# A two-network kernel at batch 1: x is loaded first and split before the decay constants, bias rows are loaded one at a time, and the last retention head is computed one weight tile earlier

## The chip, the cores and the metric

The kernel runs on one core of one Trainium2 chip. PE is the matrix engine, DVE the vector engine, ACT the scalar (activation) engine, POOL (GpSimd) and SP only issue DMAs here, apart from a few fills at the start. The metric is the device time of one execution in microseconds (us); lower is better. Of the kernel before there are three timed runs and one profiled execution.

## The reference

Two networks run one after the other on x of 256 tokens by 1024, all in float32. Cut to what the change touches:

```python
x = first_block(x, ...)    # layer 0: retention + FFN, layer 1: dilated attention + FFN
x = second_block(x, ...)   # two layers, with a recurrence whose decay is
                           # exp(-8 * r * softplus(-rg_lambda))

def retention(x, w_in, w_out):                 # 4 heads, q/k 256 wide, v 512 wide
    q, k, v, gate = split(x @ w_in)
    q, k = rope(q), rope(k) * 256 ** -0.5
    y = (q @ k.T * decay[head]) @ v            # per head, causal, over 256 tokens
    y = (y - mean(y)) * rsqrt(var(y) + 1e-5)   # over the 512 of a head
    return (silu(gate) * y) @ w_out

def dilated_attention(x, w_in, w_out, rel_bias):   # 3 groups x 16 heads of 64
    s = q @ k.T * 64 ** -0.5 + bias[group, head, distance]   # T5 buckets of rel_bias
    ...
```

`-8 * softplus(-rg_lambda)` depends on weights alone; the text calls it the decay constants (`rate` in the kernel). It is first used in the second network, some 1500 us later.

## The kernel before, in words

All weights form one stream of tiles of 512 KB (128 x 1024 float32), 878 in all, in the order of use. SP loads tile b into slot b % 4 of `raw` (L275, L297) as soon as tile b - 4 has been split. ACT rounds it to `wh` (`hi`, L397), DVE forms the rest `wl = raw - wh` (`lo`, L863), each with two buffers, and PE multiplies in three passes (high x high, high x low, low x high; L1534 to L1536), so that a float32 product comes of fast passes. `hi(b)` waits until tile b - 2 has been used on PE. Activations are split in the same way, x into `xh` and `xl`.

The order on each engine is that in which the code is written: every engine runs its own program and waits on semaphores. A piece of work that is late holds back all that is written behind it on its engine. There is no scheduler.

**Start.** POOL issues the loads of constants (`cst`, with the identity), vectors (`vec`: gains, biases, lambda) and x (L331 to L333); SP issues the first four raw tiles at once. PE transposes x in 16 pieces (L1663) and then the gain rows of `vec` (L1665), and goes on to the value tiles of retention, the first of which waits for half of `xl`. ACT splits tiles 0 and 1, takes an exponential for the decay constants and rounds x (L480). DVE begins with three tiny operations on constants and vectors, splits tiles 0 and 1, computes the decay constants in a chain of 26 operations of 128 x 4 (a series of odd powers, L971 to L981), and only then forms `xl` (L986).

**Retention heads.** The 16 gate tiles (n = 0 to 15) run through PE, and between them stand the heads' own products: `ret_scores(h)` (L1685), `ret_values(h)` (L1699, L1700) and the sum of squares `ret_var(h)` (L1708), in a period of three tiles. With them go on DVE `ret_decay` (L1026), `ret_recip` (L1031), `ret_gate` (L1036) and `ret_scale` (L1042), on ACT `ret_square` (L500) and `ret_std` (L504). For the last head DVE multiplies the products by the reciprocal as L1077 and by the gate as L1081. The output tiles that follow need all PSUM banks of the products, so PE waits for L1077 before the first of them (`r_yg`).

**Bias rows of attention.** PE forms the bias rows of all heads, POOL stores them in DRAM (L352) and loads them back head by head, shifted by one per partition (L358, 384 KB each), into four buffers. The first four loads wait only for the store and for the norm before; each later one waits for a used buffer (`a_b`). Meanwhile 24 value tiles of the attention stage pass through PE; they are loaded in pieces of 1 KB. The first bias is used after the tile at offset 30 of the stage.

Of the kernel before, what the change touches and what calls it, by code (L numbers as in the profile page):

```python
# [93 lines left out]
def build(nc, stream, x_in, consts, ret_c, att_c, vecs, rg_w, keys, scratch, out):  # L94
    with ExitStack() as ctx:
# [121 lines left out]
        const_in, x_in_s, retc_in, attc_in = sem("const_in"), sem("x_in"), sem("retc_in"), sem("attc_in")  # L217
# [55 lines left out]
        def _(sp):  # L273
# [18 lines left out]
            def in_parts(first, parts):  # L292

                for b, (g, part) in enumerate(parts, first):
                    if b >= 4:
                        sp.wait_ge(w_lo, b - 3)
                    sp.dma_start(raw[:, b % 4, :].rearrange("p (m n) -> p m n", m=4),  # L297
# [32 lines left out]
        def _(pool):  # L330
            pool.dma_start(cst[:, :], consts).then_inc(const_in, 16)  # L331
            pool.dma_start(vec[:, :], vecs).then_inc(const_in, 16)
            pool.dma_start(xr[:, :, :], x_in.rearrange("(c p) d -> p c d", p=P)).then_inc(x_in_s, 16)  # L333
            pool.wait_ge(x_turned, 1)
# [20 lines left out]
            for h in range(AH):  # L355
                if h >= 4:
                    pool.wait_ge(a_b, h - 3)
                pool.dma_start(bs[:, h % 4, :, :], bass.AP(  # L358
                    scratch.tensor, h * 384, [[1, P], [AH * 384, G3], [1, T]])).then_inc(b_in[h % 4], 16)
# [20 lines left out]
        def _(act):  # L380
# [92 lines left out]
            act.wait_ge(const_in, 32)  # L473
            hi(0)
            hi(1)
            act.wait_ge(sp_abs, 1)
            A(spw[:, 2, :], spw[:, 1, :], ACT.Exp, scale=-1.0).then_inc(sp_exp, 1)
            act.wait_ge(x_turned, 1)
            for g in range(4):
                A(xh[:, 2 * g:2 * g + 2, :], acc[:, 2 * g:2 * g + 2, :], ACT.Copy).then_inc(x_hi, 1)  # L480
            act.wait_ge(rows_in_vec, 1)
            A(vec_rows[0:104, :], ps_x[0:104, 0, 0:P], ACT.Copy).then_inc(rows_copied, 1)

# [23 lines left out]
            for n in range(16):  # L507
                hi(RET_G + n + 2)
                evacuate(RET_G + n, 16 + n, sg[:, n, :], ACT.Silu)
                if n >= 3 and n % 3 == 0 and n < 15:  # L510
                    ret_square(n // 3 - 1)
                elif n >= 4 and n % 3 == 1 and n < 15:
# [334 lines left out]
        def _(dve):  # L847
# [115 lines left out]
            dve.wait_ge(const_in, 32)  # L963
# [4 lines left out]
            lo(0)  # L968
            lo(1)
# [13 lines left out]
            for g in range(4):  # L983
                dve.wait_ge(x_hi, g + 1)
                b = slice(2 * g, 2 * g + 2)
                V.tensor_tensor(xl[:, b, :], acc[:, b, :], xh[:, b, :].bitcast(F32), ALU.subtract).then_inc(x_lo, 1)  # L986
# [62 lines left out]
            for n in range(16):  # L1049
# [3 lines left out]
                elif n in (2, 5, 8, 11):  # L1053
# [16 lines left out]
                elif n == 12:  # L1070
                    ret_gate(2)
                    ret_scale(2)
                elif n == 14:
                    ret_recip(3)
                elif n == 15:
# [452 lines left out]
        def _(pe):  # L1528
# [130 lines left out]
            pe.wait_ge(const_in, 32)  # L1659
# [545 lines left out]
```

## Time and profile before

| | us |
|---|---|
| median of 3 timed runs | 2948.59 |
| lowest and highest | 2946.07, 2948.68 |
| the profiled execution | 2945.24 |
| its span (first to last instruction) | 2943.5 |
| PE busy | 2817.1 (96%) |
| DVE busy, ACT busy | 1941.7, 1557.4 |
| mean granted clock of PE | 0.989 |

The page gives an engine's busy time, the chain of work that ended last, and groups of instructions by line. A timeline row is one or several equal instructions in a row, with the idle time before them in brackets and what ended it. A released wait is put down to the last event that was needed. The granted clock is a share of 2.4 GHz; it has two levels here, 1.0 and 0.5.

### The profile page before, as it was taken

Reading aid. Unit: us, or ns where it says so; the run is one execution under the profiler, and the core shown is the slowest. Engines: PE = TensorE matmul, PEld = TensorE weight load, DVE = VectorE, ACT = ScalarE, POOL = GpSimd, SP = SyncE. Lnnn points to the kernel's source line nnn. Section 1 sums busy time; section 2 is a strip of 40 time slices with the busy share of each in tenths; the row PEclk is TensorE's granted clock in tenths of the full one; section 3 lists DMA queues with packets and bytes.
Section 4 is the critical chain, followed back from the end, with each engine's and each line's share of the span. In section 5 each row is a group of like instructions: output and inputs, shape, how many; then the busy total and the mean of one; then the engine's idle time right before and its main releaser. Section 6 shows DMA issues by size and latency. Waiting matters only on the chain.

```text
span 2943.5 us, 51574 instructions
## 1 busy us (share of the span) xinstructions
PE 2817.1 (96%) x18787; PEld 2548.3 (87%) x18787; DVE 1941.7 (66%) x3107; ACT 1557.4 (53%) x2815; POOL 23.0 (1%) x38
## 2 busy tenths in 40 slices
PE   8999999999999989999999999998999999999998
PEld 6988987898898879999998888887999999978886
DVE  5656454555555869986886555568799678855555
ACT  4455453555545564446775444456544577644444
POOL 0000000000000000000000000000000000000000
PEclk9999999999999999999999999999999999999999
DMA  6435556664554444454444555543444444455554
GB/s 219 151 130 183 185 170 180 172 159 149 165 184 159 133 130 164 158 170 143 138 144 144 192 190 189 191 161 109 163 161 163 159 140 143 138 178 192 190 189 149
DMA packets 158659, 480.26 MB, mean 163 GB/s; under 512 B 14608, under 2 KB 51472, under 8 KB 158128
## 3 DMA queue, kind: packets, MB, share of 16 engines
q1 hardware_dynamic: 154080, 460.38, 47.4%
q0 software_dynamic: 4432, 17.87, 2.6%
q8 instruction: 98, 1.61, 0.2%
q14 instruction: 49, 0.40, 0.0%
HBM read 477.02 MB, written 1.18 MB: 162 GB/s over the span
## 4 chain that ended last, share of the span: by engine, by line
PE 77%; DVE 16%; ACT 4%; issue 2%; DMA 1%; POOL 0%; DVEq 0%; ACTq 0%; POOLq 0%
PE ps L1534 23%; PE ps L1536 23%; PE ps L1535 23%; DVE wl L863 6%; PE ps L2049 4%; ACT wh L397 2%; DVE arena L1251 1%; DVE mh L1404 1%; DVE picks L1406 1%; DVE mh L1398 1%; PE ps L1653 1%; DMA raw<-stream_dram 1%; DVE xr L882 0%; PE ps L2015 0%; DVE picks L1428 0%
## 5 line engine op out<-in xcount | busy, mean ns | idle before, releaser
L863 DVE TENSOR_TENSOR wl<-raw,wh 128x1024 fp32r<-128x1024 f32 x878 | 1075.5, 1225 | 889.6 <-ACT wh L397 883.6
L397 ACT ACTIVATE wh<-raw 128x1024 fp32r<-128x1024 f32 x878 | 929.9, 1059 | 1281.8 <-PE ps L1536 1270.9
L1534 PE MATMUL ps<-xh,wh 128*128 128x256 f32 x3920 | 1138.9, 291 | 24.4 <-DVE wl L863 22.9
L1535 PE MATMUL ps<-xl,wh 128*128 128x256 f32 x3920 | 1111.5, 284 | 0.0
L1536 PE MATMUL ps<-xh,wl 128*128 128x256 f32 x3920 | 1110.9, 283 | 0.0
L1534 PEld LDWEIGHTS ps<-xh,wh 128*128 128x128 f32 x3920 | 753.4, 192 | 49.2 <-issue 36.9
L1535 PEld LDWEIGHTS ps<-xl,wh 128*128 128x128 f32 x3920 | 754.6, 193 | 0.4
L1536 PEld LDWEIGHTS ps<-xh,wl 128*128 128x128 f32 x3920 | 753.7, 192 | 0.0
L1534 PE MATMUL ps<-wh,mh 128*128 128x512 f32 x1304 | 516.6, 396 | 13.7 <-DVE ml L875 8.8
L1536 PE MATMUL ps<-wh,ml 128*128 128x512 f32 x1304 | 512.1, 393 | 0.0
L1535 PE MATMUL ps<-wl,mh 128*128 128x512 f32 x1304 | 511.0, 392 | 0.0
L1534 PEld LDWEIGHTS ps<-wh,mh 128*128 128x128 f32 x1304 | 246.0, 189 | 90.9 <-issue 33.3
L1536 PEld LDWEIGHTS ps<-wh,ml 128*128 128x128 f32 x1304 | 246.0, 189 | 54.2
L1535 PEld LDWEIGHTS ps<-wl,mh 128*128 128x128 f32 x1304 | 246.7, 189 | 43.5
L411 ACT ACTIVATE arena<-ps 128x256 f32<-128x256 f32 (+1 forms) x360 | 132.2, 367 | 0.2
L1534 PE MATMUL ps<-wh,xh 128*128 128x512 f32 x248 | 101.4, 409 | 15.5 <-DVE wl L863 5.7
L875 DVE TENSOR_TENSOR ml<-arena,mh 128x512 fp32r<-128x512 f32 x158 | 108.1, 686 | 4.4 <-ACT mh L443 4.4
L443 ACT ACTIVATE mh<-arena 128x512 fp32r (+1 forms) x158 | 96.9, 615 | 7.1 <-DVE arena L1494 3.9
L1494 DVE TENSOR_TENSOR arena<-arena,ps 128x260 f32<-128x260 f32 (+42 forms) x128 | 71.1, 556 | 42.7 <-ACT arena L817 40.9
L1535 PE MATMUL ps<-wl,xh 128*128 128x512 f32 x248 | 98.8, 398 | 0.0
L1536 PE MATMUL ps<-wh,xl 128*128 128x512 f32 x248 | 98.4, 397 | 0.0
L797 ACT ACTIVATE picks<-mh,pickT 128x128 f32<-128x128 f32 x256 | 81.5, 398 | 4.4 <-DVE mh L1482 4.4
(280 smaller groups left out, 2040.1 us busy)
## 6 DMA issues: line engine op xcount, KB each, us to landing
raw<-stream_dram SPq DMA_DIRECT2D x878, 512.0 KB, 3.3
arena<-bias_scratch POOLq DMA_DIRECT2D x16, 384.0 KB, 9.8
arena<-norm_rows POOLq DMA_DIRECT2D x4, 1024.0 KB, 6.8
arena<-keys_dram POOLq DMA_DIRECT2D x2, 1024.0 KB, 5.1
arena<-ret_c_dram POOLq DMA_DIRECT2D x1, 1344.0 KB, 6.1
xr<-x_dram POOLq DMA_DIRECT2D x1, 1024.0 KB, 9.2
out_dram<-arena POOLq DMA_DIRECT2D x2, 512.0 KB, 2.9
arena<-rg_w_dram POOLq DMA_DIRECT2D x2, 256.0 KB, 2.9
```

The source lines that it names most:

```text
L397: A(wh[b % 2][:, :, :], raw[:, b % 4, :].rearrange("p (a b) -> p a b", a=DB), ACT.Copy) \
L411: A(dst, src, func, scale=scale, **kw).then_inc(evac, 1)
L443: A(mh[:, s:s + 2, :], src, ACT.Copy).then_inc(m_hi, 1)
L797: ins = A(gated[n % 3][:, j, :], oh[n % 2][:, j, :].bitcast(F32), ACT.Copy, scale=gT[:, t:t + 1])
L863: V.tensor_tensor(wl[b % 2][:, :, :], raw[:, b % 4, :].rearrange("p (a b) -> p a b", a=DB), wh[b % 2][:, :, :].bitcast(F32), ALU.subtract) ...
L875: V.tensor_tensor(ml[:, s:s + 2, :], src, mh[:, s:s + 2, :].bitcast(F32), ALU.subtract) \
L1251: ins = V.scalar_tensor_tensor(out=cy[:, b, :], in0=src, scalar=vec[:, w:w + 1], in1=cy[:, b, :], op0=ALU.mult, op1=ALU.add)
L1494: V.tensor_tensor(h, h, ps_a[:, n % 4, :].rearrange("p (t m) -> p m t", t=4)[:, 0:known, :], ALU.mult).then_inc(g_mul, 1)
L1534: M(out_ap, lh, rh, start=first, stop=False, skip_group_check=skip)
L1535: M(out_ap, lh, rl, start=False, stop=False, skip_group_check=skip)
L1536: return M(out_ap, ll, rh, start=False, stop=last, skip_group_check=skip)
L2049: ins = M(ps_a[:, n % 4, j * P:(j + 1) * P], gated[n % 3][:, j, :], oh[n % 2][:, 4 + j, :].bitcast(F32), start=True, stop=True)
```

## The change

Three parts.

1. x is the first load that POOL issues, the vectors the second; ACT issues the constants. Raw tiles 2 and 3 wait until x has landed. PE transposes x block by block (both token halves of a block of 128 columns in turn) and signals after each pair of blocks; ACT and DVE split x pair by pair. DVE splits tiles 0 and 1 first, then does its three small operations, then `xl`, and then the decay constants. The retention constants are loaded after the whole transposition, as before. Constants and vectors have semaphores of their own.
2. The first four bias loads wait for the split of tile 12, 16, 20 and 24 of the attention stage (counted from its start).
3. For the last retention head, scores, decay, products, square, variance, deviation, reciprocal and product stand one gate tile earlier than before.

```diff
@@ SP
                     if b >= 4:
                         sp.wait_ge(w_lo, b - 3)
+                    elif b == 2:
+                        sp.wait_ge(x_in_s, 16)
@@ POOL
-            pool.dma_start(cst[:, :], consts).then_inc(const_in, 16)
-            pool.dma_start(vec[:, :], vecs).then_inc(const_in, 16)
             pool.dma_start(xr[:, :, :], x_in.rearrange("(c p) d -> p c d", p=P)).then_inc(x_in_s, 16)
-            pool.wait_ge(x_turned, 1)
+            pool.dma_start(vec[:, :], vecs).then_inc(vec_in, 16)
+            pool.wait_ge(x_turned, 4)
             pool.dma_start(rc, ret_c).then_inc(retc_in, 16)
...
                 if h >= 4:
                     pool.wait_ge(a_b, h - 3)
+                else:
+                    pool.wait_ge(w_lo, START["att"] + 12 + 4 * h)
@@ ACT
-            act.wait_ge(const_in, 32)
+            act.dma_start(cst[:, :], consts).then_inc(const_in, 16)
             hi(0)
             hi(1)
-            act.wait_ge(sp_abs, 1)
-            A(spw[:, 2, :], spw[:, 1, :], ACT.Exp, scale=-1.0).then_inc(sp_exp, 1)
-            act.wait_ge(x_turned, 1)
             for g in range(4):
+                act.wait_ge(x_turned, g + 1)
                 A(xh[:, 2 * g:2 * g + 2, :], acc[:, 2 * g:2 * g + 2, :], ACT.Copy).then_inc(x_hi, 1)
             act.wait_ge(rows_in_vec, 1)
             A(vec_rows[0:104, :], ps_x[0:104, 0, 0:P], ACT.Copy).then_inc(rows_copied, 1)
+            act.wait_ge(sp_abs, 1)
+            A(spw[:, 2, :], spw[:, 1, :], ACT.Exp, scale=-1.0).then_inc(sp_exp, 1)
...
-                if n >= 3 and n % 3 == 0 and n < 15:
-                    ret_square(n // 3 - 1)
-                elif n >= 4 and n % 3 == 1 and n < 15:
+                if n in (3, 6, 9, 11):
+                    ret_square((n - 1) // 3)
+                elif n in (4, 7, 10, 12):
                     ret_std(n // 3 - 1)
@@ DVE
+            lo(0)
+            lo(1)
+            dve.wait_ge(const_in, 16)
+            dve.wait_ge(vec_in, 16)
...
-            lo(0)
-            lo(1)
+            for g in range(4):
+                dve.wait_ge(x_hi, g + 1)
+                b = slice(2 * g, 2 * g + 2)
+                V.tensor_tensor(xl[:, b, :], acc[:, b, :], xh[:, b, :].bitcast(F32), ALU.subtract).then_inc(x_lo, 1)
             dve.wait_ge(sp_exp, 1)
...
-            for g in range(4):
-                dve.wait_ge(x_hi, g + 1)
-                b = slice(2 * g, 2 * g + 2)
-                V.tensor_tensor(xl[:, b, :], acc[:, b, :], xh[:, b, :].bitcast(F32), ALU.subtract).then_inc(x_lo, 1)
...
-                elif n in (2, 5, 8, 11):
+                elif n in (2, 5, 8, 10):
                     ret_decay(n // 3)
...
-                elif n == 14:
+                elif n == 13:
                     ret_recip(3)
-                elif n == 15:
+                elif n == 14:
                     y3 = ry[:, 12:16, :]
...
@@ PE
-            for c in range(NC_T):
-                for b in range(DB):
+            for b in range(DB):
+                for c in range(NC_T):
                     ins = nc.tensor.transpose(acc[:, b, c * P:(c + 1) * P], xr[:, c, b * P:(b + 1) * P], ident)
-            ins.then_inc(x_turned, 1)
+                if b % 2:
+                    ins.then_inc(x_turned, 1)
+            pe.wait_ge(vec_in, 16)
             nc.tensor.transpose(ps_x[0:104, 0, 0:P], vec[:, 0:104], ident).then_inc(rows_in_vec, 1)
...
-                if n >= 4 and n % 3 == 1:
+                if n in (4, 7, 10, 12):
                     ret_var(n // 3 - 1)
-                elif n >= 3 and n % 3 == 0 and n < 15:
-                    ret_values(n // 3 - 1)
-                elif n >= 2 and n % 3 == 2 and n < 14:
+                elif n in (3, 6, 9, 11):
+                    ret_values((n - 1) // 3)
+                if n in (2, 5, 8, 10):
                     ret_scores(n // 3)
```

What stands in a row on the engines follows, with the waits of each instruction in brackets; "x3" is three equal instructions. Line numbers of the kernel after differ a little: L863 is L866 there.

On DVE, at the start, before: the end of the decay constants (L979 to L981), the four pieces of `xl` (L986), and the weight splits from tile 2 on (L863).

```order
L979 TENSOR_TENSOR arena<-arena 128x4 [waits dve_step]
L980 TENSOR_SCALAR arena<-arena 128x4 [waits dve_step]
L981 SCALAR_TENSOR_TENSOR rate<-arena 128x4 [waits dve_step]
L986 TENSOR_TENSOR xl<-ps,xh 128x512 [waits x_hi,dve_step]
L986 TENSOR_TENSOR xl<-ps,xh 128x512 [waits x_hi] x3
L863 TENSOR_TENSOR wl<-raw,wh 128x1024 [waits w_hi] x4
```

After: tiles 0 and 1 (L866), the three small operations (L970 to L973), the four pieces of `xl` (L977), and the first of the decay constants.

```order
L866 TENSOR_TENSOR wl<-raw,wh 128x1024 [waits w_hi] x2
L970 TENSOR_TENSOR head_rows<-cst 128x8 [waits vectors_in,const_in]
L972 TENSOR_SCALAR arena<-vec 128x4
L973 TENSOR_TENSOR arena<-arena,vec 128x4 [waits dve_step]
L977 TENSOR_TENSOR xl<-ps,xh 128x512 [waits x_hi] x4
L979 TENSOR_SCALAR arena<-arena 128x4 [waits rate_exp]
L980 RECIPROCAL arena<-arena 128x4 [waits dve_step]
L981 TENSOR_TENSOR arena<-arena 128x4 [waits dve_step]
```

And where the decay constants end, the weight split of tile 2 follows them:

```order
L987 TENSOR_TENSOR arena<-arena 128x4 [waits dve_step]
L988 TENSOR_SCALAR arena<-arena 128x4 [waits dve_step]
L989 SCALAR_TENSOR_TENSOR rate<-arena 128x4 [waits dve_step]
L866 TENSOR_TENSOR wl<-raw,wh 128x1024 [waits w_hi,dve_step]
L866 TENSOR_TENSOR wl<-raw,wh 128x1024 [waits w_hi] x3
```

So `xl` has moved ahead of the chain, and the split of tile 2 (L866, waiting on `dve_step`, the chain's own semaphore) now stands right behind it.

On DVE at the last gate tiles, before: the weight splits of steps n = 10 and 11 (L863 x2; step n splits the tile two ahead, gate tile n + 2), and so on to L1081, the product with the gate of the last head.

```order
L863 TENSOR_TENSOR wl<-raw,wh 128x1024 [waits w_hi] x2
L1026 TENSOR_TENSOR arena<-ps,arena 128x384 [waits ret_y,ret_scores]
L1031 RECIPROCAL arena<-arena 128x256 [waits ret_std]
L863 TENSOR_TENSOR wl<-raw,wh 128x1024 [waits w_hi,dve_step]
L1036 TENSOR_TENSOR arena<-ps,arena 128x1024 [waits evac,ret_y]
L1042 TENSOR_TENSOR arena<-arena 128x1024 [waits ret_gated]
L863 TENSOR_TENSOR wl<-raw,wh 128x1024 [waits w_hi] x2
L1031 RECIPROCAL arena<-arena 128x256 [waits ret_std]
L863 TENSOR_TENSOR wl<-raw,wh 128x1024 [waits w_hi,dve_step]
L1077 TENSOR_TENSOR arena<-ps,arena 128x1024
L1081 TENSOR_TENSOR arena<-arena 128x1024 [waits ret_gated,evac]
```

After, from the last head's decay (L1030, before L1026) on; L1035 is the reciprocal, L1081 and L1085 are the two products of the last head (before L1077 and L1081).

```order
L1030 TENSOR_TENSOR arena<-ps,arena 128x384 [waits ret_y,ret_scores]
L866 TENSOR_TENSOR wl<-raw,wh 128x1024 [waits w_hi]
L1035 RECIPROCAL arena<-arena 128x256 [waits ret_std]
L866 TENSOR_TENSOR wl<-raw,wh 128x1024 [waits w_hi,dve_step]
L1040 TENSOR_TENSOR arena<-ps,arena 128x1024 [waits evac,ret_y]
L1046 TENSOR_TENSOR arena<-arena 128x1024 [waits ret_gated]
L866 TENSOR_TENSOR wl<-raw,wh 128x1024 [waits w_hi]
L1035 RECIPROCAL arena<-arena 128x256 [waits ret_std]
L866 TENSOR_TENSOR wl<-raw,wh 128x1024 [waits w_hi,dve_step]
L1081 TENSOR_TENSOR arena<-ps,arena 128x1024
L866 TENSOR_TENSOR wl<-raw,wh 128x1024 [waits w_hi]
L1085 TENSOR_TENSOR arena<-arena 128x1024 [waits ret_gated,evac]
```

The last head's decay stands before the split of step 11 instead of behind it, its reciprocal before the split of step 14 (gate tile 16, which is the first output tile) instead of behind it, and its first product before the split of step 15 (tile 17) instead of behind it.

On POOL around the bias rows, before: the store of the rows (L352), the 16 loads (L358), and the gain rows of the next norms (L339).

```order
L352 DMA bias_scratch<-arena 16x3x384 [waits bias_vec_copied]
L358 DMA arena<-bias_scratch 128x3x256 [waits norm_updated,bias_stored]
L358 DMA arena<-bias_scratch 128x3x256 x3
L358 DMA arena<-bias_scratch 128x3x256 [waits att_biased] x12
L339 DMA arena<-norm_rows 128x2x1024 [waits att_biased,norm_updated]
```

After:

```order
L353 DMA bias_scratch<-arena 16x3x384 [waits bias_vec_copied]
L361 DMA arena<-bias_scratch 128x3x256 [waits w_lo,norm_updated,bias_stored]
L361 DMA arena<-bias_scratch 128x3x256 [waits w_lo] x3
L361 DMA arena<-bias_scratch 128x3x256 [waits att_biased] x12
L340 DMA arena<-norm_rows 128x2x1024 [waits att_biased,norm_updated]
```

The first four loads have each got a wait on the weight splits (`w_lo`); the order is the same.

## Rows read from the trace of the kernel before

**Rows 1.** The page: span, and the chain that ended last by engine.

```profile
span 2943.5 us, 51574 instructions
...
PE 77%; DVE 16%; ACT 4%; issue 2%; DMA 1%; POOL 0%; DVEq 0%; ACTq 0%; POOLq 0%
```

**Rows 2.** Timeline, 0 to 20 us: start, duration, engine, line, operation [idle before, releaser].

```profile
1.28 0.70 POOL L331 DMA_DIRECT2D cst<-consts_dram  x1 [0.83 <-POOLq L2197]
...
2.52 0.73 POOL L333 DMA_DIRECT2D xr<-x_dram  x1
...
11.72 0.16 DVE L971 TENSOR_SCALAR arena<-arena 128x4 f32<-128x4 f32 x1
...
11.86 3.65 PE L1663 MATMUL ps<-cst,xr 128*128 128x128 f32 x16 [11.86 <-DMA xr<-x_dram]
...
15.55 2.07 ACT L480 ACTIVATE xh<-ps 128x512 fp32r<-128x512 f32 x4 [5.09 <-PE ps L1663]
...
16.66 0.16 DVE L981 SCALAR_TENSOR_TENSOR rate<-arena 128x4 f32<-128x4 f32 x1
...
16.85 2.48 DVE L986 TENSOR_TENSOR xl<-ps,xh 128x512 fp32r<-128x512 f32 x4
...
18.29 0.47 PE L1534 MATMUL ps<-wh,xh 128*128 128x512 f32 x1 [2.56 <-DVE xl L986]
```

**Rows 3.** Timeline of PE, 22.3 to 28 us: third tile's first product.

```profile
25.46 0.40 PE L1534 MATMUL ps<-wh,xh 128*128 128x512 f32 x1
```

**Rows 4.** DMA, 0 to 60 us: GB/s in slices; loads, KB, us to landing.

```profile
GB/s 0 165 377 380 361 393 389 349 321 204 175 115 366 432 40 44 360 287 308 176 212 180 172 219 140 268 104 307 96 268 107 245 136 216 253 102 307 98 279 57
...
xr<-x_dram POOLq DMA_DIRECT2D x1, 1024.0 KB, 9.2
...
arena<-norm_rows POOLq DMA_DIRECT2D x1, 1024.0 KB, 5.4
```

**Rows 5.** Groups of PE by line: count, busy us, mean ns, idle before.

```profile
L1818 PE MATMUL ps<-cst,arena 128*128 128x128 f32 x16 | 4.4, 273 | 0.0
...
L1663 PE MATMUL ps<-cst,xr 128*128 128x128 f32 x16 | 3.6, 423 | 11.9 <-DMA xr<-x_dram 11.9
```

**Rows 6.** Stretches: busy (count) of PE, PEld, DVE, ACT, POOL; clock, DMA, GB/s.

```profile
189.84:193.26 3.42, 3.24 (x8) 2.59 (x9) 1.30 (x2) 0.00 (x0) 0.00 (x0) 0.51 0.47 153
...
479.97:483.40 3.43, 3.43 (x8) 2.76 (x9) 1.63 (x2) 0.07 (x1) 0.00 (x0) 0.51 0.53 170
```

**Rows 7.** Timeline, 184 to 191 us: the last head and the first output tile.

```profile
185.76 1.75 DVE L1031 RECIPROCAL arena<-arena 128x256 f32<-128x256 f32 x1
...
187.56 1.23 DVE L863 TENSOR_TENSOR wl<-raw,wh 128x1024 fp32r<-128x1024 f32 x1
...
188.70 1.22 DVE L1077 TENSOR_TENSOR arena<-ps,arena 128x1024 f32<-128x1024 f32 x1
...
190.02 0.76 PE L1534 MATMUL ps<-wh,mh 128*128 128x512 f32 x1 [3.71 <-issue]
```

**Rows 8.** Timeline, 455 to 500 us: bias loads, and the value tiles of attention.

```profile
460.88 3.01 POOL L358 DMA_DIRECT2D arena<-bias_scratch  x4 [3.12 <-DMA bias_scratch<-arena]
...
479.92 0.80 PE L1534 MATMUL ps<-wh,xh 128*128 128x512 f32 x1 [5.73 <-DVE wl L863]
...
485.70 1.23 DVE L863 TENSOR_TENSOR wl<-raw,wh 128x1024 fp32r<-128x1024 f32 x1 [4.11 <-ACT wh L397]
...
488.42 1.23 DVE L863 TENSOR_TENSOR wl<-raw,wh 128x1024 fp32r<-128x1024 f32 x1 [1.49 <-ACT wh L397]
```

**Rows 9.** DMA, 460 to 480 us: queues (packets, MB, share); raw tiles' landing.

```profile
q0 software_dynamic: 456, 1.58, 40.1%
...
q1 hardware_dynamic: 2614, 2.60, 39.9%
...
raw<-stream_dram SPq DMA_DIRECT2D x6, 512.0 KB, 11.1
```

**Rows 10.** DMA, 545 to 575 us: raw tiles' landing.

```profile
raw<-stream_dram SPq DMA_DIRECT2D x7, 512.0 KB, 3.8
```

More of the change, by code:

```diff
@@ L216, in build @@
         m_hi, m_lo = sem("m_hi"), sem("m_lo")
-        const_in, x_in_s, retc_in, attc_in = sem("const_in"), sem("x_in"), sem("retc_in"), sem("attc_in")
+        const_in, vec_in, x_in_s, retc_in, attc_in = sem("const_in"), sem("vectors_in"), sem("x_in"), sem("retc_in"), sem("attc_in")
         x_turned, x_hi, x_lo = sem("x_turned"), sem("x_hi"), sem("x_lo")
@@ L960, in norm @@
                         updated(c)
-            dve.wait_ge(const_in, 32)
+            lo(0)
+            lo(1)
+            dve.wait_ge(const_in, 16)
+            dve.wait_ge(vec_in, 16)
             V.tensor_tensor(head_rows[:, :], ident[:, 0:H2], ident[:, 32:32 + H2], ALU.add).then_inc(rows_in, 1)
@@ L1072, in _ @@
                     ret_scale(2)
+                elif n == 13:
+                    ret_recip(3)
                 elif n == 14:
-                    ret_recip(3)
-                elif n == 15:
                     y3 = ry[:, 12:16, :]
@@ L1656, in norm @@
                             ins.then_inc(n_turned, 1)
-            pe.wait_ge(const_in, 32)
+            pe.wait_ge(const_in, 16)
             pe.wait_ge(x_in_s, 16)
-            for c in range(NC_T):
-                for b in range(DB):
+            for b in range(DB):
+                for c in range(NC_T):
                     ins = nc.tensor.transpose(acc[:, b, c * P:(c + 1) * P], xr[:, c, b * P:(b + 1) * P], ident)
-            ins.then_inc(x_turned, 1)
+                if b % 2:
+                    ins.then_inc(x_turned, 1)
+            pe.wait_ge(vec_in, 16)
             nc.tensor.transpose(ps_x[0:104, 0, 0:P], vec[:, 0:104], ident).then_inc(rows_in_vec, 1)
```

## The prediction

> **What bounds the kernel now.** I read the page first: its chain of work that ended last lies on PE for 77% of the span and on DVE for 16%, and the profiled execution has a span of 2943.5 us [rows 1]. So only time in which PE stands still, or runs at half its clock, can be won here; nothing in the change takes a product away. Then I read the timelines at the three places that the change touches, with the DMA view beside them.
>
> At the start x lands at 2.52 + 9.2 = 11.7 us, PE transposes from 11.86, and its first product against weights begins at 18.29, released by the split of x on DVE. That split (xl, 16.85) stands behind a chain of tiny operations, the decay constants (11.72 to 16.82, 5.1 us). The third weight tile begins at 25.46 [rows 2, 3]. At the end of the retention stage PE waits 3.71 us, until 190.02, for the last head's product L1077 on DVE, which stands behind a reciprocal and a weight split [rows 7]. In the attention stage PE waits 5.73 us, until 479.92, for a weight split whose raw tile was late: four loads of bias rows had gone out together at 460.88, and raw tiles issued in that stretch took 11.1 us to land, against 3.8 later [rows 8 to 10]. Behind both waits lie 3.4 us at a granted clock of 0.51, which is the level of 1.2 GHz, half of 2.4 [rows 6].
>
> **The change, part by part.**
>
> *x first.* Before x has landed, 4 raw tiles of 512 KB, 328 KB of constants, 138 KB of vectors and 1024 KB of x are moved: 3538 KB, 3.62 MB. The slices of 1.5 us show 361 to 393 GB/s [rows 4]; at 380 that is 9.5 us, and with the first bytes at about 2.2 us it gives 11.7, as measured. Now raw tiles 2 and 3 wait for x, so 2376 KB (2.43 MB) stand before it: 6.4 us, 8.6. The vectors now follow x and may share its last stretch (0.14 MB, 0.4 us). I take 8.9. Bounds: with the issue alone moved (from 2.52 to 1.28, where the constants' issue stood [rows 2]) and nothing of the crowd gone, 10.5; with no crowd at all, 1.28 + 5.4 (the 1024 KB load of the gain rows [rows 4]) = 6.7.
>
> Some edits here I cost at nothing. The constants' load is issued by ACT, which otherwise waits for the first raw tile; it has 4 us before PE wants it. Raw tiles 2 and 3 go out at 9 and land by about 13 to 14, and nobody can use them before tile 0 is done, at 15.6 or later. Queued behind the waiting issue on SP are tiles 4 and 5, which are wanted after 20. The 1344 KB load of the retention constants follows the last transposition as before. The vectors gate the first DVE operation after the weight splits and the last transposition; they must be there by about 10.5, else the whole split of x moves with them.
>
> *The split before the decay constants.* From x at 8.9: 16 transpositions 3.65 us [rows 2], 9.0 to 12.65. ACT and DVE now follow in four pieces (0.52 and 0.62 us each, from 2.07 and 2.48 for four [rows 2]); the last piece ends on ACT at 13.2 and on DVE at 13.95. PE begins tile 0 at 12.9, after the turned vectors. On ACT a copy of the vector rows (104x128) and an exponential (128x4) follow, both small beside its 0.52. Then DVE runs the decay constants, 14.0 to 19.1, and only behind them the low half of tile 2, 1.23 us, 20.3. Tiles 0 and 1 are done at 12.9 + 2 x 2.72 = 18.4 (2.72 is one tile: 488.42 - 485.70 [rows 8]). So tile 2 begins at 20.4 instead of 25.46 [rows 3]: the start gains 5.1 us, and a new wait of about 2 us stands where the chain was moved to. Without it the gain would be 7.1.
>
> The 16 transpositions have a mean of 423 ns, the same form later 273 [rows 5], so the start is at the low level. If tile 0 is too, it costs up to 1.7 us, but inside the wait of 2 us, nothing. The Trainium skill, "TensorE: Matmul & The Clock Gate", Part 1, says that the throttled clock is the default and that activity releases it, and that the phase differs from run to run. The two means agree; by that rule the remaining wait may be followed by a slow stretch in some executions and not in others.
>
> *The last head one tile forward.* Scores, products and variance of head 3 go behind tiles 10, 11 and 12 instead of 11, 12 and 13. PE does the same work up to 186.3. On DVE the reciprocal (1.75 us, 185.76 [rows 7]) moves ahead of tile 16's split, and L1077 takes the place at 185.76; it takes 1.22, so PE can begin at about 187.1. The wait shrinks from 3.71 to 0.8: 2.9 us. With a wait of 0.8 the half-clock stretch should go: 190.02 to 193.26 at half is 3.24 us that do the work of 1.6. Sum 4.5. What is late next: tile 17's split keeps its 187.56 to 188.8 [rows 7], and the second output tile wants it at 187.1 + 2.72 = 189.8; it holds. Bounds: 0 if the moved reciprocal meets a late variance, 5.3 if L1077 is ready when PE is.
>
> *Bias rows one by one.* The four loads took 40.1% of 20 us of all 16 DMA engines, 2.0 us each [rows 9]. A raw tile is asked for when the split four tiles earlier is done, 1.23 us after that split began; ACT wants it 1.1 us before its own split begins. Four tiles are 10.9 us, so it has 10.9 - 1.2 - 1.1 = 8.6 us to land. With 11.1 it was late; with 3.8 to 4 [rows 10] and one bias load of 2.0 in its way it takes about 6. One load in four tiles also fits in sum: 2.0 + 4 x 1.6 (a raw tile's share, from 2.60 MB in 39.9% of 20 us [rows 9]) = 8.4 of 10.9 us. The first row set is loaded 18 tiles before its use, the fourth 6 tiles, 16 us. So the wait of 5.73 goes and with it the half-clock stretch, 3.43 us that do 1.7: 7.4 us. Bounds: if the four still make raw tiles late by a little each, I keep half, 3.7; more than 7.4 isn't there.
>
> **Sum.** 5.1 + 4.5 + 7.4 = 17.0, less 0.8 for half a chance of a slow stretch behind the new wait at 20.4: 16.2. Against the profiled execution, 2945.24 (span 2943.5 and 1.7 around it), that is 2929.0; the median of the runs shown is 3.35 higher, 2948.59, which gives 2932.4. I take 2931.
>
> **The rivals.** *x lands without a crowd*, at 6.7: everything at the start, the decay chain too, comes 2.2 earlier, 2929. For it: ACT and SP use one queue kind and x another. Against: the 9.2 us it took in company. The Trainium skill, "DMA: Bandwidth & Descriptors", Anatomy of one DMA, fits a load from this queue as 2.0 us and the bytes at 436 GB/s, 4.4 for x; by it alone x would be there at 5.7 and the whole come to about 2928 (an estimate from that page), and only the 5.4 row comes near it.
>
> *The head's wait only moves.* Two groups of products now stand behind tile 10, and DVE has decay, reciprocal, product and scaling within three tiles. If one of these makes PE wait as long as before, 4.5 is lost: 2935.5. Against it: DVE's work between two of these tiles is 3 to 4 us, and the tiles with products behind them are 4.5 to 6 us apart.
>
> *The attention wait stays or is spread* over the four bias loads: 3.7 to 7.4 are lost, 2935 to 2938.
>
> *Slower: each bias load stalls PE for itself.* If one load of 2.0 us among raw tiles makes the tile behind it land later than 8.6 us, and each of the four does what the group did, that is 4 x 7.4 = 29.6 in place of the one 7.4 gone: 2960. It decides at 8.6 us of landing. Against it is the 3.8 while bias loads went out in pairs [rows 10]. If it is only one of four, the time is about 2938.
>
> *x isn't earlier than its issue* (10.5, or the vectors late): 1.6 less, 2932.5; it lies inside my forecast's scatter.
>
> **How the numbers follow.** Forecast (both x cases at the start included) 0.66, its own range 2926 to 2936. x without a crowd 0.08. Head's wait moves 0.09. Attention wait stays or is spread 0.12. Slower 0.05. The range of 8 in 10: from 2925 (all three waits gone and x early) to 2940 (the attention gain lost, from the higher median: 2932.4 + 7.4). 0.2% is 5.9 us, about what a measurement of this kernel can tell from no change. Faster by more, under 2942.7: all but the last case and a rest for two terms failing together, 0.90; within, 0.06; slower, 0.04.
>
> **What would show it.** In the profile after: x landing near 8.9; the first weight product near 12.9; a wait of about 2 us at the third tile, released by a weight split that follows the decay chain; at the output tiles of retention a wait under 1 us, with the clock at 1.00; no wait of PE over 1 us in the value tiles of attention, and raw tiles landing under 8.6 us there. Wrong would be the forecast if x lands after 10.5, if PE waits between gate tiles 10 and 14, or if the value tiles have waits on a weight split behind each bias load.

## The result, and the profile after

The kernel after takes 2930.48 us (median of 4 runs, 2929.25 to 2931.00) against 2947.33 of the kernel before (4 runs, 2945.87 to 2948.68) on the same chip: the ratio is 0.9942, with a 95% interval of 0.9931 to 0.9954, or 16.9 us. Forecast were 2931, and faster by 16.2 us. The two profiled executions are 2945.24 and 2930.42 us, 14.8 apart.

The page of the kernel after:

```profile
span 2928.6 us, 51574 instructions
...
PE 77%; DVE 16%; ACT 4%; issue 2%; DMA 1%; DVEq 0%; ACTq 0%; POOL 0%; POOLq 0%
```

It answers to [rows 1]: the shares of the chain are the same to the percent, and only the span has shrunk, by 14.9 us. A gain of 0.5% isn't seen in shares; it is seen where rows of one and the same piece of work are set side by side.

The timeline of the kernel after at the start, against [rows 2, 3] (start, duration, engine, line, operation; idle before and its end in brackets):

```profile
1.29 0.85 POOL L333 DMA_DIRECT2D xr<-x_dram  x1 [0.83 <-POOLq L2203]
...
9.47 3.65 PE L1667 MATMUL ps<-cst,xr 128*128 128x128 f32 x16 [9.47 <-DMA xr<-x_dram]
...
12.98 0.78 PE L1538 MATMUL ps<-wh,xh 128*128 128x512 f32 x1
...
14.39 0.16 DVE L979 TENSOR_SCALAR arena<-arena 128x4 f32<-128x4 f32 x1
...
19.33 0.16 DVE L989 SCALAR_TENSOR_TENSOR rate<-arena 128x4 f32<-128x4 f32 x1
19.52 2.36 DVE L866 TENSOR_TENSOR wl<-raw,wh 128x1024 fp32r<-128x1024 f32 x2
...
20.80 0.50 PE L1538 MATMUL ps<-wh,xh 128*128 128x512 f32 x1 [1.70 <-DVE wl L866]
```

x is issued at 1.29, PE transposes from 9.47 instead of 11.86, the first weight product comes at 12.98 instead of 18.29 and the third tile at 20.80 instead of 25.46. In front of it stands the new wait, 1.70 us, on the weight split at 19.52, and that follows the end of the decay constants (19.33) directly. In the kernel before the first tile had run for the most part at half clock, behind the wait of 2.56 us, and had taken 4.41 us (18.29 to 22.70):

```profile
19.12:22.54 3.42, 3.42 (x10) 2.65 (x9) 0.21 (x1) 0.00 (x0) 0.21 (x1) 0.50 0.61 251
```

Now it takes 3.24 us. The 4.7 us of the start are thus 5.3 at the first product and 1.2 in the first tile, less the new wait of 1.7 and 0.1. DMA in the first 60 us, against [rows 4]:

```profile
GB/s 0 170 379 384 396 388 6 255 381 343 354 416 430 165 105 321 283 303 261 338 304 170 297 107 299 61 294 159 193 145 206 236 141 270 115 281 46 322 197 156
...
xr<-x_dram POOLq DMA_DIRECT2D x1, 1024.0 KB, 8.1
...
cst<-consts_dram ACTq DMA_DIRECT2D x1, 328.0 KB, 3.2
```

The seventh slice (9 to 10.5 us) moves next to nothing: SP issues its third raw tile only at 9.35, when x is there, and POOL waits for the transposition. x took 8.1 us in place of 9.2.

The end of retention in the kernel after, against [rows 7]; L1035 is the reciprocal, L1081 the first product of the last head:

```profile
178.67 1.75 DVE L1035 RECIPROCAL arena<-arena 128x256 f32<-128x256 f32 x1
...
180.47 1.23 DVE L866 TENSOR_TENSOR wl<-raw,wh 128x1024 fp32r<-128x1024 f32 x1
...
181.61 1.22 DVE L1081 TENSOR_TENSOR arena<-ps,arena 128x1024 f32<-128x1024 f32 x1
...
182.93 0.47 PE L1538 MATMUL ps<-wh,mh 128*128 128x512 f32 x1 [0.49 <-issue]
```

The wait of PE is 0.49 us instead of 3.71. The stretch behind it, of which [rows 6] show the like before, is at full clock:

```profile
182.93:186.30 3.37, 3.37 (x15) 2.78 (x16) 2.36 (x2) 1.21 (x3) 0.00 (x0) 1.00 0.50 159
```

The attention stage, POOL's issues and then PE, against [rows 8]:

```profile
465.77 0.79 POOL L361 DMA_DIRECT2D arena<-bias_scratch  x1 [16.38 <-DVE wl L866]
476.75 0.76 POOL L361 DMA_DIRECT2D arena<-bias_scratch  x1 [10.19 <-DVE wl L866]
487.73 0.76 POOL L361 DMA_DIRECT2D arena<-bias_scratch  x1 [10.22 <-DVE wl L866]
498.83 0.76 POOL L361 DMA_DIRECT2D arena<-bias_scratch  x1 [10.34 <-DVE wl L866]
```

```profile
508.13 1.06 ACT L400 ACTIVATE wh<-raw 128x1024 fp32r<-128x1024 f32 x1 [2.59 <-DMA raw<-stream_dram]
...
510.50 0.50 PE L1538 MATMUL ps<-wh,xh 128*128 128x512 f32 x1 [0.64 <-DVE wl L866]
```

The four loads now stand 11 us apart and the wait of 5.73 us is gone. One of 0.64 is left, behind the fourth load: the raw tile of 508.13 came late (ACT waited 2.59 us for it). Issued at 498.55, 0.3 us before the fourth bias load, it took 9.6 us. Raw tiles of 490 to 510 us landed after 6.7 us (median of 7), between the 11.1 of [rows 9] and the 3.8 of [rows 10].

**Where the 14.9 us of the profiled pair lie.** One fixed point is POOL's first pair of later bias loads, issued when two heads have used theirs: 548.45 before, 533.56 after:

```profile
548.45 1.49 POOL L358 DMA_DIRECT2D arena<-bias_scratch  x2 [84.55 <-DVE arena L1157]
```

```profile
533.56 1.51 POOL L361 DMA_DIRECT2D arena<-bias_scratch  x2 [33.98 <-DVE arena L1161]
```

The kernel after is 14.9 us ahead there, as much as at its end. In between the distance isn't constant: it goes up to 18.5 and down to 13.7, mostly in steps of about 1.5 us (more on them under order_only). Set side by side by the order number of the PE product, the two traces give the steps: 4.7 at the third tile, 4.2 from tile 14 on (a wait of 0.25 us has come there), 8.5 behind the retention stage, 15.9 behind the big attention wait, 14.9 at the fixed point.

### The profile page after: what moved, and what is told of

Read it like the earlier page. It is cut to its first block, busy times and chain, and to the rows that moved or that the text cites. A ratio compares the mean times of both kernels' runs of the same rounds, so it can differ in the third digit from the quotient of the medians.

```text
span 2928.6 us, 51574 instructions
## 1 busy us (share of the span) xinstructions
PE 2813.6 (96%) x18787; PEld 2545.0 (87%) x18787; DVE 1941.9 (66%) x3107; ACT 1557.9 (53%) x2815; POOL 22.7 (1%) x37
## 4 chain that ended last, share of the span: by engine, by line
PE 77%; DVE 16%; ACT 4%; issue 2%; DMA 1%; DVEq 0%; ACTq 0%; POOL 0%; POOLq 0%
PE ps L1538 23%; PE ps L1540 23%; PE ps L1539 23%; DVE wl L866 6%; PE ps L2055 4%; ACT wh L400 2%; DVE arena L1255 1%; DVE mh L1408 1%; DVE picks L1410 1%; DVE mh L1402 1%; DVE xr L885 0%; PE ps L2021 0%; DVE picks L1432 0%; DVE picks L1440 0%; DVE picks L1423 0%
## 5 line engine op out<-in xcount | busy, mean ns | idle before, releaser
L866 DVE TENSOR_TENSOR wl<-raw,wh 128x1024 fp32r<-128x1024 f32 x878 | 1075.6, 1225 | 881.6 <-ACT wh L400 875.1
L1538 PE MATMUL ps<-wh,mh 128*128 128x512 f32 x1304 | 515.2, 395 | 10.5 <-DVE ml L878 8.8
```

What stands on the lines that cost most here:

```text
L866: V.tensor_tensor(wl[b % 2][:, :, :], raw[:, b % 4, :].rearrange("p (a b) -> p a b", a=DB), wh[b % 2][:, :, :].bitcast(F32), ALU.subtract) ...
L1538: M(out_ap, lh, rh, start=first, stop=False, skip_group_check=skip)
```

## The experiments

All run against the kernel before on their own chip. The medians scatter by some us (those of the kernel before are 2947.33, 2948.33, 2949.90 and 2950.81), so beside each ratio I give the place in the profiled execution at which the edit acts.

**only_start, only_head, only_bias: each part alone.** The kernel before with one of the three parts of the diff shown above, and nothing else.

> The kernel before with part 1 alone (x first, raw tiles 2 and 3 behind x, split before the decay constants). Theory (the three gains are separate and add up): the third weight tile begins at 20.8 us as in the kernel after instead of 25.46, 0.4 of the 4.7 us is lost by tile 14, so the time is 4.2 us under the kernel before; the waits at the head (3.7 us) and in the attention values (5.7 us) stay as they were. Rival (the start sets the phase of everything that follows, and much of the 16.9 us hangs on it): over 8 us faster, with one of the two later waits changed by more than 1 us.

> The kernel before with part 3 alone (last head one tile earlier). Theory: the wait before the first output tile of retention falls from 3.71 to 0.5 to 0.8 us and the half-clock stretch behind it goes; 4.3 to 4.5 us faster. Rival (the half-clock stretch hangs on the time since the start and not on the wait): the wait goes and the stretch stays, 2.9 us faster.

> The kernel before with part 2 alone (each of the first four bias loads behind a weight split). Theory: the wait of 5.73 us and the 3.4 us at half clock behind it go, 7.4 us, of which 1.0 comes back as small waits near the fourth load: 6.4 us faster. Rival (in the kernel after some of this gain came from the other parts, since the stage begins 8.5 us earlier there): under 4 us faster, with a wait over 2 us left in the value tiles.

Ratios 0.9988 (0.9979 to 0.9997), 0.9978 (0.9968 to 0.9988) and 0.9977 (0.9968 to 0.9986): 3.5, 6.5 and 6.8 us, each with an interval of nearly 3 us to either side, sum 16.8, against 17.1 for all three by 0.9942. The places, in this order: PE at the third tile in only_start, PE at the first output tile in only_head, and all waits of PE in the stretch of 440 to 545 us in only_bias.

```profile
20.67 0.50 PE L1536 MATMUL ps<-wh,xh 128*128 128x512 f32 x1 [1.29 <-DVE wl L864]
```

```profile
186.86 0.47 PE L1534 MATMUL ps<-wh,mh 128*128 128x512 f32 x1 [0.49 <-issue]
```

```profile
PE ps L1804 <- DVE arena L1153: 0.7, 1, 0.7
PE ps L1791 <- DVE arena L997: 0.3, 1, 0.3
```

The start gives 4.8 us at the third tile and 4.4 at the end of its stage; the waits at 181.9 (3.72 us) and 469.6 (4.60) stay in only_start. The head's wait falls to 0.49, and no half-clock stretch follows: 4.3 us are won over that stage. In only_bias no wait on a weight split is left in the value tiles; 7.6 us are won over them, and 0.5 given back. Over their own stages the three are 4.4, 4.3 and 7.6 us, against 4.2, 4.3 and 7.6 in the kernel after: the gains are separate and add up. At the fixed point the three kernels are 5.1, 4.4 and 7.6 us ahead, 2.2 more in sum than the kernel after; of these, 0.8 came to only_start behind its own stage, and 1.2 is what the kernel after gives back behind the retention stage. The rivals fall, with one exception in part: in only_start the wait in the attention values was 1.1 us shorter than before, with the same loads, so the size of that wait itself varies from execution to execution.

**bias_together_late: four loads at once, but later.**

```diff
-                    pool.wait_ge(w_lo, START["att"] + 12 + 4 * h)
+                    pool.wait_ge(w_lo, START["att"] + 12)
```

> The kernel after, but all four first bias loads wait for the same split, that of tile 12 of the attention stage, and so go out together 17 us later than in the kernel before. Theory (four at once crowd out the raw tiles, whenever it is): a PE wait of 4 to 6 us returns behind them, with half clock behind it, raw tiles land after 10 us; 6 to 7 us slower than the kernel after, about 2937. Rival (what helped was that the loads no longer fall on the first value tiles, right behind the store of the rows): no wait over 1 us, the time of the kernel after, 2930.

2940.78 us in its one run. Waits of PE, 440 to 540 us, and the loads issued from 465 to 485 us:

```profile
PE ps L1538 <- DVE wl L866: 7.0, 1, 7.0
```

```profile
raw<-stream_dram SPq DMA_DIRECT2D x5, 512.0 KB, 13.1
arena<-bias_scratch POOLq DMA_DIRECT2D x4, 384.0 KB, 9.9
```

The wait is back, 7.0 us, and raw tiles took 13.1 us. It is the four together that crowd out the raw tiles, not the place in the stage. By 540 us this kernel has lost 8.3 us of the 14.9. Expected had been a wait of 4 to 6 us and about 2937: the direction was right, the price too low.

**raw_not_held: raw tiles 2 and 3 don't wait for x.**

```diff
-                    elif b == 2:
-                        sp.wait_ge(x_in_s, 16)
```

> The kernel after without the wait of raw tiles 2 and 3 on x: all four raw tiles are issued at once again, x is still POOL's first load. Theory (bytes ahead of x set its landing): 1.05 MB more at 380 GB/s, x lands 2.8 us later than the 9.4 of the kernel after, about 12.2 less what x's own turn among the queues gives back, and the third weight tile begins 2 to 2.8 us later; 2932 to 2933. Rival (x is bound by its own queue, not by the others' bytes): x lands at 9.4 as before and the time stays 2930.

2931.20 us, one run. PE in this kernel, and x's load:

```profile
10.07 3.57 PE L1665 MATMUL ps<-cst,xr 128*128 128x128 f32 x16 [10.07 <-DMA xr<-x_dram]
...
21.33 0.51 PE L1536 MATMUL ps<-wh,xh 128*128 128x512 f32 x1 [2.12 <-DVE wl L864]
```

```profile
xr<-x_dram POOLq DMA_DIRECT2D x1, 1024.0 KB, 8.6
```

x is there 0.6 us later, not 2.8, and took 8.6 us in place of 8.1, although 1.05 MB more were under way. So the sum of bytes ahead of x, on which I had the landing, isn't what sets it: x shares with the raw tiles and isn't behind all of them. The kernel before shows it too: its fourth raw tile, issued at 2.33 and counted ahead of x in the prediction, took 10.7 us and landed at 13.0, behind x. What brought x forward from 11.86 to 9.47 is mostly its place as the first load of its queue (1.23 us by the issue, 2.52 to 1.29), with 0.6 for the held tiles; the remaining 0.6, for what no longer stands ahead of it in that queue, is only what is left over. The 0.6 for the held tiles rests on one execution: in six kernels with all of part 1's loads the transposition begins between 9.33 and 9.78, in four with the old loads between 11.51 and 11.86, and 10.07 lies 0.3 outside the first group.

**order_only: the order of work alone, all loads as before.**

```diff
-            pool.dma_start(xr[:, :, :], x_in...).then_inc(x_in_s, 16)
-            pool.dma_start(vec[:, :], vecs).then_inc(vec_in, 16)
+            pool.dma_start(cst[:, :], consts).then_inc(const_in, 16)
+            pool.dma_start(vec[:, :], vecs).then_inc(vec_in, 16)
+            pool.dma_start(xr[:, :, :], x_in...).then_inc(x_in_s, 16)
```

(against only_start; ACT issues nothing and SP holds nothing back)

> The kernel before with only the order of the work at the start changed (PE signals pairs of blocks, ACT and DVE split x ahead of the decay constants), while all loads are issued where they were in the kernel before. Theory (landing of x and order of work each give about half of the start's 4.7 us): x lands at 11.7 as before, the third weight tile begins 11.4 us behind it (the distance in the kernel after), at 23.1, 2.3 us earlier than the 25.46 of before. Rival (the order alone does nothing, since the chain of 5.1 us is only moved from one tile to the next): third tile within 0.5 us of 25.46. Rival 2 (the order gives all, the landing nothing): 20.8.

PE in this kernel:

```profile
11.56 3.65 PE L1663 MATMUL ps<-cst,xr 128*128 128x128 f32 x16 [11.56 <-DMA xr<-x_dram]
...
22.88 0.50 PE L1534 MATMUL ps<-wh,xh 128*128 128x512 f32 x1 [1.50 <-DVE wl L862]
```

The third tile comes 11.32 us behind the first transposition, as in the kernel after (20.80 - 9.47 = 11.33), and at 22.88, 2.6 us earlier than before. Of these 0.3 are x's landing, which came at 11.56 instead of 11.86 although no load was moved. The distance from the transposition to the third tile fell from 13.60 to 11.32: 2.3 us by the order. The other 2.4 are x's landing (11.86 to 9.47). That is the theory's half and half. The ratio is 0.9993 (0.9984 to 1.0002), so the 2.6 us can't be told from nothing in the time. The reason stands in the line with the mean granted clock, of four kernels: before, after, order_only and, below, best1_thirds.

```profile
core 0: 2943.5 us, clock 0.989
```

```profile
core 0: 2928.6 us, clock 0.991
```

```profile
core 0: 2948.3 us, clock 0.987
```

```profile
core 0: 2924.2 us, clock 0.992
```

In this profiled execution of order_only the clock not granted comes to 1.3% of the span, 38 us, in the one of before to 1.1%, 32 us, of after 0.9%, 26 us (the last digit makes 1.5 us either way). At the fixed point, 548.57, order_only has already lost its 2.6 us again, though behind the third tile PE has only one wait up to there that before hadn't, 0.26 us at 56.6, and none that is longer by more than 0.03 us. Half-clock stretches took them. Behind the same wait of 3.7 us at the first output tile PE stays at half clock for some 6 us instead of 3.2 (granted clock 0.50 from 187.71 to 193.30), and 1.3 us are gone. Behind the same wait of 2.6 us the same 32 transpositions follow, before and in order_only:

```profile
239.34 4.24 PE L1653 MATMUL ps<-arena 128*128 128x128 f32 x32 [2.60 <-DVE arena L915]
```

```profile
238.20 5.84 PE L1653 MATMUL ps<-arena 128*128 128x128 f32 x32 [2.58 <-DVE arena L914]
```

The granted clock over them reads 1.00 before (239.34 to 243.30), and 0.50 in order_only from 238.20 to 241.40; that is another 1.6 us. The steps of 1.5 us between before and after are of this kind: behind a wait of 2.58 us at 746 in the kernel before and at 731 in the kernel after, half clock follows in the first and not in the second. What decides it isn't shown. Work of 5 us at one place is smaller than what an execution wins or loses by where half-clock stretches happen to fall.

**chain_late: the decay constants moved away.** The 26 operations go, four at a time, behind the weight splits of the query and key tiles with odd n.

```diff
+                elif n % 2:
+                    rate_part(n // 2)     # four links of the chain
```

> The kernel after with the 26 operations of the decay constants moved from behind the split of x into the query and key tiles of retention, four at a time behind every second weight split. Theory: the wait of 1.7 us before the third weight tile goes (tile 2's split then ends at about 18.8 instead of 20.75) and nothing else moves; 1.7 us faster, 0.1%. Rival (the third tile is as much held by its raw tile or by ACT): under 0.5 us. Rival 2 (the pieces make a later weight split late): slower than the kernel after by some tenths.

2930.73 us, ratio 0.9948 (0.9934 to 0.9961): no different from the kernel after. The wait of 1.70 us is gone from the trace, the third tile begins at 19.44 instead of 20.80, and at the fixed point it is 1.4 us ahead (532.18). So the new wait was what the prediction had named, with the size of 1.4 to 1.7 us; in the time this isn't seen. In the attention values a larger wait than in the kernel after has come, 1.3 us, here behind the second bias load and not the fourth (the raw tile issued 0.3 us before it took 10.2 us):

```profile
PE ps L1545 <- DVE wl L866: 1.3, 1, 1.3
```

**x_on_sp: SP issues x ahead of the raw tiles.**

```diff
+            sp.dma_start(xr[:, :, :], x_in.rearrange("(c p) d -> p c d", p=P)).then_inc(x_in_s, 16)
             in_parts(0, value_parts(RET_V, 16))
```

> The kernel after, but SP issues x, ahead of the first raw tiles, instead of POOL. Theory for x: it lands at 5 to 6 us instead of 9.4, since nothing but the constants shares the way. Theory for the time: ACT and DVE still split tiles 0 and 1 first, and raw tile 1 lands at about 8.7 as before, so the split of x follows at about the same time and the third weight tile moves by under 1 us: same time as the kernel after. Rival (x's landing is what decides): the third weight tile 3 us earlier, 2927.

2930.93 us, ratio 0.9941 (0.9928 to 0.9955). x is there at 7.4, not at 5 to 6, and the third tile comes 1.6 us later than in the kernel after (22.36):

```profile
7.38 3.65 PE L1667 MATMUL ps<-cst,xr 128*128 128x128 f32 x16 [7.38 <-DMA xr<-x_dram]
...
11.08 2.04 ACT L481 ACTIVATE xh<-ps 128x512 fp32r<-128x512 f32 x4
...
14.13 0.76 PE L1538 MATMUL ps<-wh,xh 128*128 128x512 f32 x1 [2.89 <-DVE xl L977]
...
15.12 0.63 PE L1540 MATMUL ps<-wh,xl 128*128 128x512 f32 x1
...
15.55 0.63 PE L1538 MATMUL ps<-wh,xh 128*128 128x512 f32 x1
```

Raw tiles 0 and 1 now land later and ACT, which splits them first, takes x only at 11.08; PE waits 2.89 us, and then its first tile runs at 0.43 us a product instead of 0.23, the slow level. Two expectations were off: the landing, and that nothing would get worse. At the fixed point it is 0.6 us behind the kernel after (534.13).

**best1: both, and x split in halves between the weight tiles.**

```diff
             for g in range(4):
                 act.wait_ge(x_turned, g + 1)
                 A(xh[:, 2 * g:2 * g + 2, :], ...).then_inc(x_hi, 1)
+                if g % 2:
+                    hi(g // 2)
```

> Both of the former together (x issued by SP first, decay constants in later tiles), and ACT and DVE take x in two halves with a weight split behind each: x halves 1, tile 0, x halves 2, tile 1. Theory: first weight product at about 10.5 instead of 12.98, third weight tile at 16 to 17.5 instead of 20.8 (the later, if the first tiles run at half clock), 3.3 to 4.8 us under the kernel after: 2926 to 2927. Rival (raw tiles 0 and 1 land late because x is ahead of them): third tile not before 18.5, 2 us faster at most.

2930.41 us, ratio 0.9939 (0.9925 to 0.9952). The third tile begins at 17.76, 3.0 us ahead of the kernel after, the first at 12.18 and not at 10.5, and the fixed point comes at 529.90, 3.7 ahead. In the time this isn't seen: expected were 2926 to 2927.

**bias_earlier and thirds: the microsecond that came back.** The first is the kernel after with each of the four loads four tiles earlier; the second is chain_late with each of them in three pieces.

```diff
-                    pool.wait_ge(w_lo, START["att"] + 12 + 4 * h)
+                    pool.wait_ge(w_lo, START["att"] + 8 + 4 * h)
```

```diff
+                    for g in range(G3):           # 128 KB each, one per tile
+                        pool.wait_ge(w_lo, START["att"] + 12 + 4 * h + g)
+                        pool.dma_start(bs[:, h, g, :], ...).then_inc(b_in[h], 16)
```

> The kernel after with the first four bias loads four tiles earlier each (behind the splits of tiles 8, 12, 16 and 20 of the stage). Theory (the 1.0 us that comes back after the big wait is the fourth load beside the change from value tiles to head tiles, at 509 us): it goes, 0.5 to 1 us faster than the kernel after at the end of this stage. Rival (any bias load beside the value tiles' small pieces costs some tenths, wherever it stands): the same 1 us comes back, spread over other tiles.

> The kernel with the decay constants in later tiles, and each of the first four bias loads cut into its three groups of 128 KB, one behind every split of tiles 12, 13, 14, 16, 17, 18 and so on. Theory (a single bias load holds back the raw tile beside it by up to 2 us, and the slack of 8.6 us is then just used up; in the kernel with late decay constants 1.5 us came back that way): no PE wait over 0.3 us in the value tiles, 1.5 us faster at the end of the stage than that kernel. Rival (the total engine time of the bias rows counts, not its grain): the same 1.5 us.

bias_earlier took 2931.35 us in one run; from behind the big wait on it gives nothing back (0.0 instead of 1.0 us) and reaches the fixed point at 532.15. thirds took 2931.15 us, 0.9939 (0.9926 to 0.9953), and gives nothing back either, where chain_late gave back 1.6; best1_thirds below doesn't either. Its waits of PE from 440 to 545 us, all of them outside the value tiles:

```profile
PE ps L1819 <- DVE arena L1166: 0.7, 1, 0.7
PE ps L1831 <- DVE arena L1154: 0.7, 1, 0.7
PE ps L1806 <- DVE arena L1008: 0.3, 1, 0.3
```

With both the small wait is gone, though the bytes are the same. So the rival that the total counts falls, for the pieces in two executions of two kernels. That the place alone is a cure is less certain: bias_earlier has only one execution, and what came back was 0.4 to 1.6 us in the six kernels that load whole row sets behind tiles 12 to 24, so which of the two is the better cure isn't shown.

**best1_thirds: all of it together.**

> The kernel in which SP issues x first, x is split in two halves with a weight tile behind each, and the decay constants are in later tiles, with the bias loads in thirds. Theory: at the end of the attention heads 20 us ahead of the kernel before (18.5 there without the thirds, and the 1.5 that came back); its time 3 to 5 us under the kernel after, if the slow stretches later on fall alike. Rival (the later stages give it back through where the half-clock stretches fall): 20 us ahead there, but under 2 us at the end.

2929.27 us, ratio 0.9937 (0.9924 to 0.9951), its profiled execution, the fastest of five, 2925.94. POOL's pair at the fixed point:

```profile
527.57 1.51 POOL L365 DMA_DIRECT2D arena<-bias_scratch  x2 [27.83 <-DVE arena L1173]
```

20.9 us ahead of the kernel before and 6.0 ahead of the kernel after. The intervals of the two kernels overlap almost wholly, so by the time it isn't shown to be better; by the trace of one execution it is, until 530 us. Of the 3 to 5 us under the kernel after that were expected, 1.2 are seen in the medians, as the rival had it.

## Why the prediction was right

*The start, 5.1 forecast, 4.7 measured at the third tile and 4.2 from tile 14 on.* The steps hold one by one: transpositions from 9.47 (9.0), first product 12.98 (12.9), decay constants to 19.5 (19.1), third tile 20.80 (20.4) behind a wait of 1.70 (about 2). What was mis-sized is the landing of x, 0.5 late; that the first product was in time even so is luck, since it came 3.5 us behind the first transposition and not the 3.9 that I had added up. What was wrong is the reason of the landing: the step that summed all bytes ahead of x. It gave 11.7 for before and 8.9 for after, both nearly true, but raw_not_held has the bytes of the one case and nearly the landing of the other. The first tile took 3.24 us (12.98 to 16.22) against 2.72 later, so little of it was at the low level, which I had left open. That the first tile of the kernel before had lost 1.7 us at that level isn't named in the prediction; it stands in the 25.46 from which I counted, so the sum holds it. chain_late shows the price of the chain behind the split.

*The rival that x lands without a crowd* (6.7) is refuted by 9.47, and so is the landing of 5.7 that the fit in the Trainium skill, "DMA: Bandwidth & Descriptors", Anatomy of one DMA, would give; even alone on SP's queue, ahead of every raw tile, x took until 7.4.

*The head, 4.5 forecast, 4.3 measured.* The first output tile begins 2.9 us earlier for it, as forecast, and the half-clock stretch that went with the wait gave 1.5 (1.6 forecast). The wait is 0.49 instead of 0.8, but nothing was won by that: DVE was ready when I had put it (in only_head PE begins at 186.86, with x 0.3 us early; forecast 187.1), and PE came to the wait 0.35 us later than before. The rival of a wait that only moves shows nowhere: between 150 and 182 us PE stands still for more than 0.1 us only once, for 0.12.

*Bias rows, 7.4 forecast; 7.6 gone and 1.0 come back.* bias_together_late shows the cause, the four loads at once. The estimate of 6 us of landing was right in size for the median (6.7), but the raw tile issued just before a bias load is slower, and by the median it isn't seen: 9.6 us for the one before the fourth load, over the margin of 8.6. The margin itself holds: landing less the wait of PE behind it is 9.2 before (14.9 less 5.7), 9.0 after, 8.9 in chain_late (10.2 less 1.3) and 8.9 in bias_together_late (15.9 less 7.0). That part of the rival "spread over the four loads" holds, at 1.0 us of its 3.7 to 7.4. The rival on the slower side, that each load stalls PE for itself, is refuted: its condition, a landing over 8.6 us, was met beside one load of four, and the price was 1.0 us, near the excess over the margin, and not 7.4.

*The last term, 0.8 for half a chance of a slow stretch* behind the new wait: none followed in this execution, nor in the five other profiled ones that have this wait (1.29 to 2.12 us), the granted clock behind it reading 1.00 in each. So a term of 0.8 that didn't come stands against 1.2 us that came back behind the retention stage and weren't in the sum; that they nearly cancel is luck. It is small beside what wasn't in the sum, the difference between executions in all later stages. The profiled pair is 14.8 apart, the medians 16.9; the sum of the steps at the fixed point is 14.9. What the medians have beyond it, 2 us, no step of mine explains. The terms of the trace are thus 4.2, 4.3, 7.6 and 1.2 given back, 14.9 against the 16.2 of my sum; the medians lie nearer to the 16.2 than the trace does, and that too is luck. So is the half microsecond between 2931 and 2930.48: the two bases that I had gave 2929.0 and 2932.4, and I took a value between them.

## What to carry to other kernels

When several engines wait at the start, look at which work of a queue or an engine stands ahead of the one thing that all wait for, and move what isn't needed soon, a little at a time, into stretches where its engine has room; moved in one piece it becomes the next wait. Loads of side data that go out together can push a steady stream of tiles past its slack: count the slack from the buffers (here 8.6 us), space the loads so that one alone stays under it, and look at the slowest tile beside a load, not at the median (here 9.6 us against 6.7). Removing a wait of a few us from the matrix engine can be worth a third to a half as much again (1.5 us on 2.9 at the head, 1.8 on 5.7 in attention), as the half-clock stretch behind it goes too; but a single gain under 5 us must be read at its place in the trace, since the whole time scatters by as much.

## What the runs showed that was not expected

- x, 1 MB, took 8.9 to 9.2 us when third in POOL's queue, 7.9 to 8.4 when first with two raw tiles held back, 8.6 with none held back, and 6.5 when first on SP's queue with no raw tile ahead of it. Holding back 1.05 MB of other loads was worth 0.6 us.
- Four bias loads of 384 KB together took 9.9 to 12.1 us to land (medians of five kernels), with raw tiles at 11.1 in the kernel before and 13.1 in bias_together_late (medians) and the slowest at 14.9 and 15.9. Single ones took 7.2 to 9.7 us in the kernel after. Two of them took 32.6% of 20 us of the DMA engines, 3.3 us each, against the 2.0 of [rows 9].
- The transpositions at the start have a mean of 423 ns in both kernels, the like later 272 and 273 ns, while the granted clock of that stretch reads 1.00. The lower level is the likelier reading: 16 of them begin within 3.43 us, one every 0.21 us, as the first ones behind the wait in order_only do where the clock reads 0.50 (15 within 3.20 us, 238.20 to 241.40), while the 32 of the kernel before at clock 1.00 take 3.96 us, 0.12 each. So the granted clock of the first microseconds seems not to be reliable here.
